# One round of the prompt's attention in another order on TensorE: scores, compression step, value products, then transposes

## The reference

```python
proj = rmsnorm(x) @ w_in                       # SSM input, queries, six K/V parts, gates
ssm_out, h_last = ssm_branch(u, h0)            # diagonal complex state space model + GLU
nsa_out = attend(q, gates, kv...)              # sparse attention, below
merged  = g0 * (ssm_out @ w_br_ssm) + g1 * (nsa_out @ w_br_nsa)
x = x + rmsnorm(merged @ w_out)
x = x + rmsnorm(cross_attention(rmsnorm(x)))   # 4 heads, 256 memory tokens
x = x + rmsnorm(square(relu(rmsnorm(x) @ w_up)) @ w_down)
```

```python
def nsa_compress(rows, pe, w1, w2):            # 64-token blocks of K (and V) to one row
    flat = blocks(rows + pe)                   # (blocks, kv head, 64*64)
    return gelu(flat @ w1) @ w2
o_c = softmax(q @ kcmp.T, causal by block) @ vcmp
o_s = softmax(q @ selected_k.T) @ selected_v   # top 16 blocks of 64
o_w = softmax(q @ window_k.T) @ window_v       # last 512 positions
o = g[0] * o_c + g[1] * o_s + g[2] * o_w
```

## Time and profile before

| | |
|---|---|
| time, median of 3 runs | 1305.33 us (1303.79 to 1306.81) |
| the profiled execution's own time | 1309.85 us |
| its span | 1308.2 us |
| mean granted clock of TensorE | 0.957 |
| PE busy | 1199.9 us, 92% of the span |
| DVE busy | 633.0 us, 48% |
| ACT busy | 439.5 us, 34% |

### The profile page before, as it was taken

The page is one execution under the profiler, slowest core; times in us unless marked ns, Lnnn a source line. Parts: engine busy times, 40 slices in busy tenths (PEclk is TensorE's granted clock), DMA queues, the critical chain, the costliest instruction groups (busy, mean ns, idle before and its releaser), DMA issues.

```text
span 1308.2 us, 21761 instructions
## 1 busy us (share of the span) xinstructions
PE 1199.9 (92%) x8421; PEld 1059.1 (81%) x8421; DVE 633.0 (48%) x1154; ACT 439.5 (34%) x708; POOL 167.4 (13%) x276
## 2 busy tenths in 40 slices
PE   6999898989999889899989987778999999999997
PEld 5888676667877667678869876567999999999997
DVE  3549767246665451511333744354333325667563
ACT  3000110035677441410013644342323224455551
POOL 0000021363532305000000200010000000001000
PEclk9999978989999999999998999888999999999998
DMA  6561332453563726554238342411332221321201
GB/s 182 133 205 36 125 105 76 125 138 106 131 161 116 240 65 214 173 187 154 57 101 277 102 144 103 159 62 33 97 97 87 76 97 65 98 97 65 97 1 69
DMA packets 155441, 152.34 MB, mean 116 GB/s; under 512 B 41206, under 2 KB 136787, under 8 KB 155131
## 3 DMA queue, kind: packets, MB, share of 16 engines
q1 hardware_dynamic: 146330, 123.30, 30.9%
q0 software_dynamic: 9008, 27.65, 6.7%
HBM read 142.54 MB, written 12.53 MB: 119 GB/s over the span
## 4 chain that ended last, share of the span: by engine, by line
PE 78%; DVE 8%; ACT 6%; issue 3%; SPq 2%; DMA 2%; POOL 0%; DVEq 0%; ACTq 0%
PE banks L1363 22%; PE banks L924 18%; PE banks L1588 14%; PE banks L1323 4%; PE banks L1108 4%; PE banks L1304 2%; PE banks L1068 1%; ACT rounded L1780 1%; PE banks L1143 1%; DVE rounded L2616 1%; PE banks L1222 1%; PE banks L1160 1%; SPq L600 1%; DMA upper<-in_cache_win_kv 1%; PE banks L1171 1%
## 5 line engine op out<-in xcount | busy, mean ns | idle before, releaser
L1363 PE MATMUL banks<-rounded 128*128 128x288 f32 (+1 forms) x2304 | 304.0, 294 | 24.2 <-DVE rounded L2644 12.1
L1363 PEld LDWEIGHTS banks<-rounded 128*128 128x128 f32 x2304 | 299.6, 194 | 26.1 <-DVE rounded L2644 13.0
L924 PE MATMUL banks<-arena 128*128 128x272 f32 (+1 forms) x1056 | 256.3, 404 | 7.2 <-DVEq L2024 3.3
L924 PEld LDWEIGHTS banks<-arena 128*128 128x128 f32 (+1 forms) x1056 | 202.3, 193 | 53.7 <-DVEq L2024 3.5
L1588 PE MATMUL banks<-rounded 128*128 128x272 f32 x1536 | 195.2, 290 | 3.8 <-DVE rounded L2788 3.8
L1588 PEld LDWEIGHTS banks<-rounded 128*128 128x128 f32 x1536 | 194.5, 190 | 4.4 <-issue 3.1
L2616 DVE TENSOR_TENSOR rounded<-arena,rounded 128x2048 fp32r<-128x2048 f32 x46 | 107.2, 2331 | 84.7 <-ACT rounded L1780 84.6
L2788 DVE TENSOR_TENSOR rounded<-arena,rounded 128x1088 fp32r<-128x1088 f32 x64 | 82.9, 1304 | 60.3 <-ACT rounded L1985 60.3
L1985 ACT ACTIVATE rounded<-arena 128x1088 fp32r<-128x1088 f32 x64 | 71.1, 1114 | 81.0 <-PE banks L1588 79.8
L1780 ACT ACTIVATE rounded<-arena 128x2048 fp32r<-128x2048 f32 x46 | 87.6, 1906 | 0.0
L2757 DVE TENSOR_TENSOR arena<-arena 128x288 f32<-128x288 f32 (+1 forms) x64 | 28.2, 440 | 109.9 <-ACT arena L1957 109.9
(11 more groups left out here) (424 smaller groups left out, 1464.3 us busy)
## 6 DMA issues: line engine op xcount, KB each, us to landing
arena<-in_w_up SPq DMA_DIRECT2D x16, 1024.0 KB, 5.5
arena<-in_w_down SPq DMA_DIRECT2D x16, 1024.0 KB, 5.1
arena<-in_w_in SPq DMA_DIRECT2D x13, 1024.0 KB, 8.9
upper<-in_cache_nsa_kv SPq DMA_DIRECT2D x64, 128.0 KB, 2.9
upper<-in_cache_nsa_kv POOLq DMA_DIRECT2D x64, 128.0 KB, 5.0
arena<-in_w_out SPq DMA_DIRECT2D x8, 1024.0 KB, 5.8
arena<-in_cache_mem_kv SPq DMA_DIRECT2D x16, 512.0 KB, 7.0
arena<-in_cache_nsa_kv SPq DMA_DIRECT2D x90, 64.0 KB, 2.2
```

What stands on the lines that cost most here:

```text
L924: ins = mm(bank(b + h, HALF, rows=M), lhsT(k), rhs[:, k, h * HALF:(h + 1) * HALF], start=(k == 0), stop=(k == K - 1))
L1363: ins = mm(bank(b, N), w[:, k], a[:, k, toks], start=(k == 0 and z == 0), stop=(k == K - 1 and z == 2))
```

## The change

In a round, M(i) goes from the end to behind S(i), and T(i-2) from behind S(i) to behind P(i-3). `cmp2` stays at the end of its round. The order of all other engines' instructions, every wait and every size stays. The lines of PE from L1152 on change places: P is L1164 and T is L1175 after the change, and whatever stands behind L1181 has a number that is lower by one.

```diff
-                if 2 <= i < NPAIR + 2:
-                    j = i - 2
-                    qt = PAIRS[j][0]
-                    pe.wait_ge(sem("p_scaled"), j + 1)
-                    if j >= 1:
-                        pe.wait_ge(sem("pT_ready"), j)
-                    for g in range(2):
-                        for kt in range(qt + 1):
-                            ins = pe.transpose(bank(4 + g, P, kt * P), p_sb[:, j % 2, g, kt * P:(kt + 1) * P], ident)
-                    signal(ins, "p_T")
+                u, k = i // 8, i % 8
+                if i < 8 * CU and k < 7:
+                    cmp1(u, CMP_STEP[k], CMP_STEP[k + 1])
                 if i >= 3:
                     j = i - 3
...
                     signal(ins, "pv_done")
-                if i < 8 * CU:
-                    u, k = i // 8, i % 8
-                    if k < 7:
-                        cmp1(u, CMP_STEP[k], CMP_STEP[k + 1])
-                    else:
-                        cmp2(u)
+                if 2 <= i < NPAIR + 2:
...
+                    signal(ins, "p_T")
+                if i < 8 * CU and k == 7:
+                    cmp2(u)
```

More of the change, by code:

```diff
@@ L1173, in _ @@
                     signal(ins, "pv_done")
-                if i < 8 * CU:
-                    u, k = i // 8, i % 8
-                    if k < 7:
-                        cmp1(u, CMP_STEP[k], CMP_STEP[k + 1])
-                    else:
-                        cmp2(u)
+                if 2 <= i < NPAIR + 2:
+                    j = i - 2
+                    qt = PAIRS[j][0]
+                    pe.wait_ge(sem("p_scaled"), j + 1)
+                    if j >= 1:
+                        pe.wait_ge(sem("pT_ready"), j)
+                    for g in range(2):
+                        for kt in range(qt + 1):
+                            ins = pe.transpose(bank(4 + g, P, kt * P), p_sb[:, j % 2, g, kt * P:(kt + 1) * P], ident)
+                    signal(ins, "p_T")
+                if i < 8 * CU and k == 7:
+                    cmp2(u)
                 if i == NPAIR:
```

## The result

The changed kernel takes 1334.56 us (median of 4 runs, 1331.62 to 1341.64), the kernel before 1305.51 beside it. The ratio is 1.0231 with a 95% interval of 1.0186 to 1.0277: 24 to 36 us slower. The forecast was 1324.0 us, with a range of 1315.5 to 1330.5. So the direction and the waits were right and the size was too small, by 10.6 us. Two runs stand far apart and are left out of the ratios, though not out of the medians: one of the kernel before, 1400.28 us (beside e9 to e11), and one of e10, 5026.52 us.

The account below looks back on a forecast made before the run. TensorE, busy 92% of the span, was taken as the bound. Waits of 16.1 us plus 2.6 us of clock made 18.7 us, on a median of 1305.3 us: 1324.0 us, range 1315.5 to 1330.5.

Parts of the forecast that it names:

- The bound: Whole kernel: TensorE, busy 92% of the span, sets the end; a wait added to it adds time unless another goes.
- What T no longer waits for: Rounds of the stage: T's two waits for DVE's scaled probabilities inside the rounds go, 1.0 us off, between 0 and 1.8.
- M(8u+3) and the copy: Round 8u+3, units 1 to 3: M waits for ACT's last rearranging copy behind C(8u), 3 x 3.2 = 9.6 us.
- The gelu: Round 8u+7, all four units: `cmp2` waits for ACT's gelu, late behind C(8u+4) and E(8u+6), 7.0 us in all.
- The end: From round 32: ACT reaches E(31) late, and P(30) and P(31) stand closer behind their transposes; 0.5 us, between 0 and 1.5.
- The sum of the waits: Stage of the change: 9.6 + 7.0 + 0.5 - 1.0 = 16.1 us added.
- The clock: Behind the three 3.2 us gaps: two of three bring TensorE's lower clock at 1.3 us each, 2.6 us, between 0 and 3.9.
- B: Rival: the clock falls at every gap, also the four of 1.85 us, each costing more; 27.3 us, 1332.6 us; chance 0.10.
- A: Rival: only the rearranging copies bite, ACT has the gelus done in time; 11.7 us slower, 1317.0 us; chance 0.08.
- C: Rival: T no longer waits for DVE and TensorE's idle time falls to about 1 us; 2.5 us faster, 1302.8; chance 0.03.
- D: Rival: waits added and removed cancel within 0.2% (2.6 us), with two of the three copies early; chance 0.02.

Follow-up runs that it names:

- e9: The changed kernel itself, unaltered, measured again in a later set: 1335.74 us, ratio 1.0206 to the kernel before.
- e11: The changed kernel with unread filling products ahead of S(8u+3) in units 1 to 3 and ahead of P(30) and P(31): 1327.69 us, ratio 1.0136 to before.
- e10: The changed kernel with TensorE's order of before in rounds 32 to 34 alone: 1328.55 us, ratio 1.0150 to the kernel before.
- e1: The changed kernel with ACT's last rearranging copy of each unit moved one iteration earlier, ahead of C(8u): 1319.92 us, ratio 1.0103 to the kernel before.
- e5: The kernel before with the new order only in rounds 8u+2 and 8u+3 of units 1 to 3: 1319.94 us, ratio 1.0093 to the kernel before.
- e2: The changed kernel with TensorE's order of before in rounds 8u+2: 1328.76 us, ratio 1.0146 to the kernel before.
- e6: The kernel before with the new order only in rounds 6, 14, 22 and 30: 1311.08 us, ratio 1.0036 to the kernel before.
- e3: The changed kernel with TensorE's order of before in rounds 6, 14, 22 and 30: 1324.07 us, ratio 1.0112 to the kernel before.
- e7: The changed kernel with the order of before in rounds 8u+2, 8u+6 and from 32 on: 1315.48 us, ratio 1.0060 to the kernel before.
- e8: The kernel before with all of ACT's rearranging copies one iteration earlier: 1306.95 us, ratio 1.0010 to the kernel before.
- e4: The changed kernel with seven unread products of 256 columns ahead of S(8u+3) in units 1 to 3: 1329.99 us, ratio 1.0179 to the kernel before.

## Why the prediction was wrong, step by step

**The bound.** Right. TensorE's path sets the end, and what was added to its waits came out in the time.

**What T no longer waits for.** Right: 1.0 us off was charged; the two waits inside the rounds went.

**M(8u+3) and the copy.** Right: 3 x 3.2 = 9.6 us forecast, 3.31 + 3.43 + 3.31 = 10.05 measured. e1 and e5 show that it comes from this order and not from late rows. What the prediction didn't have is that unit 1 has the row loads as a second limit right behind (e2); it does not change the sum of the change itself.

**The gelu.** Right: 7.0 us forecast. `cmp2` waited for 1.62, 1.62 and 1.53 us in units 0, 2 and 3, and P(8u+4) for 0.27 in each of them; in unit 1 one wait of P for DVE, 1.84 us, stands in the place of both. That is 7.4 us in all, against 1.3 before, so 6.1 net. e6 has 5.5.

**The end.** 0.5 us forecast; its waits are 1.59 + 0.69 + 0.48 = 2.76 us against 0.78 + 0.56 = 1.34, so 1.4, in the range of 0 to 1.5. I had named ACT's lateness, but not that DVE's taking of bank 7 stands behind its scaling of pair 31.

**The sum of the waits.** 16.1 us forecast, 20.2 - 3.7 = 16.5 measured, and 16.9 in e9.

**The clock. This is the step that failed.** It was charged at 3 x 2/3 x 1.3 = 2.6 us, and 3.9 was its bound. In the stage the rest grew by 6.5 us (e9: 8.8), and the part behind the stage by 4.1 (3.6). The 6.5 us are, from the rows: M and P behind the three long gaps 5.9 us (1.58, then 1.84 + 0.89, then 1.12 + 0.45), T(13), `cmp2` and S(16) behind the wait of P(12) 1.6, less 1.6 for the stretch of round 10, which this trace doesn't have; 0.6 is small things. The term was mis-sized in three ways. First, the chance: behind gaps of 3.3 us M(8u+3) was long in 14 of 15 cases (the rows of the changed kernel, e9, e10, e3 and e5), not in two of three. Second, the price: I took it from T and P in the earlier trace rows, 1.3 us, and gave it to M. M(8u+3) lost 0.8 to 1.8 us by itself in the 14 cases, and P behind it up to 0.9 more. Third, the places: I charged only the three long gaps. The wait of P(12), 1.84 us, is followed by a loss of 1.5 to 1.6 us in four of the seven traces that have it. The 1.62 us at `cmp2` of unit 0 cost as much in e9 (S(8) 1.86 for 1.13, M(8) 3.38 for 2.50). And the two groups behind the stage lost 5.9 us, where I had put the boundary of the argument.

The stretch behind the small products of round 10 comes and goes in either order, so it is no sure cost of the change. With the new order in round 10, M(10) took 4.55 to 5.04 us in seven of eight traces, and 2.70 in the changed kernel's first. With the old order T(8) and P(7) take it in the kernel before, they and M(10) in e6 and e7, and none in e2 and e8.

e4 and e11 show the cause for the long gaps: with them filled, M(11), M(19) and M(27) are at their full rate.

Of the 10.6 us that were missing, the waits are 0.4, the clock of the stage 3.9 and the part behind it 4.1. The other 2 us are more than the two traces show; the medians have them, and they stay open.

The Trainium skill's warning (TensorE: Matmul & The Clock Gate, Why this matters for your kernels), which the prediction set against the trace, holds in 14 of 15 of these gaps. It was a better guide than the two of three that the rows of the kernel before gave.

**The rivals.** B had part of the mechanism, and its 1332.6 us is nearest to the measured 1334.56. I gave it 0.10. That it comes so near is in part luck: in the trace the clock fell behind four of its seven gaps, not behind the three of 1.5 to 1.6 us at `cmp2`, and much of the rest of the loss lies behind the stage, where B had nothing. A, C and D are refuted by the waits for L1721 and L1694.

What stays open: the part behind the stage varied between 865.8 and 873.2 us in the 13 traces, though its program is the same. In e11 it is 873.2 with both first groups at the full rate, so the 4.1 us there can't be put down to the end of the stage alone. Nor is it known why gaps of 1.6 us at `cmp2` are followed by a long M(8) in six of eight traces and never by a long M(24), or why the same three waits at the end cost 5.9 us in one trace and nothing in e4.

## What to carry to other kernels

When work is moved on the critical engine, look at what the other engines have in order behind the consumer of that work: here a copy that needed only 1 us itself had a 2 us copy and a table load with two activations behind it, and they were what TensorE needed next. Count a new idle gap of some 3 us on TensorE at its length plus the lower clock of whatever stands behind it, with the price taken from that very group, and follow it over the boundary of the stage. Where a queue is late by a known amount, put right one place at a time and look for the second limit behind the first.

## What the runs showed of the hardware

- Gaps of 3.3 to 3.4 us in an otherwise full stage were followed by the lower level in 14 of 15 cases. Shorter ones were mixed: those of 1.9 to 2.0 us (e2, e7) in one of four, that of 1.84 us at P(12) in four of seven, those of 1.5 to 1.6 us at `cmp2` in six of eight in unit 0 and in none of 16 in units 2 and 3, and the two of 1.3 and 1.5 us (e1) not.
- Products that nobody reads, issued in a gap, kept the clock: 14 records of 256 columns took 3.19 us, and the groups behind ran at 2.02 to 2.12 us in 6 of 6 cases.
- At the lower level 22 records of M took 5.04 us instead of 2.72, and 16 records of P 1.98 instead of 1.09, about in the ratio of the two clock levels.
- An activation table load (1.28 us) started 0.01 to 0.02 us behind the activation ahead of it, and the gelu 0.01 to 0.02 us behind the load, in every unit of the changed kernel.
